# The norm ahead of the last feed-forward part: squares added on GpSimd, two sums on TensorE

## The chip, the cores and the metric

The kernel runs on one core of a Trainium2 chip. The time is the device time of one execution in microseconds. It runs as one program: TensorE (matrix products), VectorE, ScalarE, GpSimd (called POOL in the profile) and the DMA queues work side by side and wait for each other by semaphores that the code sets by hand.

## The reference, cut to what matters

Two transformer blocks on 512 tokens of 1024 features. The last part of the second block is what the change touches:

```
def rms_norm(x, g):
    y = x * rsqrt(mean(x * x, axis=-1) + 1e-6)
    return y * g

x = x + rms_norm(mem_attention(h, mem_n, ...), xa_post_g)     # "xapost"
h = rms_norm(x, ffn_pre_g)                                    # "ffnpre"
x = x + rms_norm(conv_ffn(h, w_up, conv_w, conv_b, w_down), ffn_post_g)

def conv_ffn(h, w_up, conv_w, conv_b, w_down):                # D_FF = 2816
    z = h @ w_up
    zc = conv_w[2] * z + conv_w[1] * shift_right(z, 1) + conv_w[0] * shift_right(z, 2) + conv_b
    g, u = zc[..., :D_FF], zc[..., D_FF:]
    return (gelu(g) * u) @ w_down
```

Everything is float32. The sum of squares over the 1024 features of each token, needed by "ffnpre", is what is computed in another way.

## The kernel before, in words

Activations lie with features on the partitions: eight tiles k = 0 to 7 of 128 features by 512 tokens (`xT[:, k, :]`). A float32 product is made of three products of rounded parts: weights and activations are each split into a high part (a rounded copy, made by ScalarE) and a low part (the value less the high part, made by VectorE), and TensorE multiplies high by high, high by low and low by high (lines 2422 to 2424, and 3288 to 3290). Weights come in units of 128x1024, loaded by the SP queue into four buffers `raw`, split by ScalarE (`hi`, line 587) and VectorE (`lo`, line 1382) into three buffers `whi` and `wlo`. A unit's buffer is free again when TensorE has used the unit three places before it.

The norm ahead of the feed-forward part is not applied before the product: TensorE multiplies `x * g`, and the factor rsqrt(mean) of each token is applied to the result in PSUM (`times_root`, on VectorE), when it is known. To have work early, the first four column blocks of `w_up` ("f2w", four PSUM banks) are done in 16 pieces, each one feature tile k of one half of the tokens (256 columns). `wide_order` is the order: tiles 0 to 5 of the first half, tiles 0 to 3 of the second, tiles 6 and 7 of the first, tiles 4 to 7 of the second. For piece n:

- VectorE: `half_norm(n)`, line 2126 (y1 times its gain times the factor of "xapost") and line 2128 (added to xT);
- ScalarE: `half_high(n)`, line 1278 (high part `h5h`) and line 1282 (square of xT into `tmp[k % 4]`). The square of a tile k >= 4 waits until the square four tiles before it in its half has been read (semaphore `p_sq`);
- VectorE: `half_low(n)`, line 2134 (low part `h5l`);
- TensorE: `half_wide(n)`, twelve products of 256 columns (3 for each of the four banks), and then line 3296, a product of a 128x128 matrix of ones with the square. It adds the squares over the 128 features of the tile, and over the eight tiles by accumulating in the bank "ffnpre". It raises `p_sq`, the last one `p_sum`.

The order in each engine's queue is written out by hand. On VectorE weight splits (`lo`) and the two steps of the second "xapost" factor (`newton`, lines 1394 and 1396) stand between the pieces; on ScalarE the weight copies (`hi`) and the roots. A matrix product with a float32 `ones` is issued as two instructions.

Before the pieces TensorE fills the four banks and the "ffnpre" bank with zeros by a product (line 3274), since every later product accumulates. Behind the pieces it goes on with the blocks ("f2g", jj) and ("f2u", jj), jj = 2 to 10, eight feature tiles of three products of 512 columns each. When `p_sum` is raised, ScalarE's `root("ffnpre")` (lines 601, 603, 609) and VectorE's `newton` make the factor, and then for each hidden block jj VectorE multiplies by it (line 2080), both engines compute the convolution (lines 1312, 2180, 2183), the gelu (1317), the product (2208) and the two parts of the result (1322, 2210), with weight splits in between.

`acc` is a 128x512 buffer in which VectorE has added squares for the two "xapost" sums; TensorE has read each half of it when `p_sum` stands at "xapost0" or "xapost1". GpSimd's last work is the scaling of the memory attention's probabilities (line 2396), before this stretch.

Of the kernel before, what the change touches and what calls it, by code (L numbers as in the profile page):

```python
# [12 lines left out]
ALU = mybir.AluOpType  # L13
# [181 lines left out]
def build(nc, ap, out):  # L195
# [4 lines left out]
    job = Order(JOBS)  # L200

    with ctx:
        def sem(name):
            return ctx.enter_context(nc.semaphore(name))
# [9 lines left out]
        def fix(name, shape, dt=F32):  # L214
            nonlocal o
            n = int(np.prod(shape)) * (1 if dt == U8 else 4)
            t = place(name, shape, dt, o)
            o += (n + 63) // 64 * 64
            return t
# [3 lines left out]
        ones = fix("ones", [128])  # L223
# [17 lines left out]
        tmp = [fix(f"tmp{i}", [512]) for i in range(4)]  # L241
# [9 lines left out]
        def work(name, shape, dt, kb):  # L251
            assert kb * KB + int(np.prod(shape)) * 4 <= WN, (name, kb, WN / KB)
            return place(name, shape, dt, W0 + int(kb * KB))
# [4 lines left out]
        def bank(b, n=512, c=0):  # L258
            return pall[:, 512 * b + c:512 * b + c + n]
# [71 lines left out]
        acc = work("acc", [512], F32, 124)  # L331
# [57 lines left out]
        s = Sems(*[sem("s_" + n) for n in Sems._fields])  # L389
# [54 lines left out]
        at = {n: i % 8 for i, n in enumerate(fills)}  # L444
# [71 lines left out]
        half_of = (slice(0, 256), slice(256, 512))  # L516
# [5 lines left out]
        wide_order = [(0, k) for k in range(6)] + [(1, k) for k in range(4)] + [(0, 6), (0, 7)] + [(1, k) for k in range(4, 8)]  # L522
# [1743 lines left out]
        def _(e):  # L2266
# [125 lines left out]
            for i in range(1, 16, 2):  # L2392
# [2 lines left out]
                w.wait_ge(s.drec, 64 + i + 1)  # L2395
                e.tensor_scalar(p, p, sd[:, c + 3:c + 4], None, ALU.mult).then_inc(s.pwg, 1)

        @block.tensor
        def _(e):
            w = Waits(e)  # L2400
            freed = {b: [] for b in range(8)}

            def fill(b):

                for sem_, value in freed[b]:
                    w.wait_ge(sem_, value)

            def unit(j):
                _, _, _, cn, _, nk, _ = plan[j]
                w.wait_ge(*lo_done(j))  # L2410
                return [t[j % 3][:, 0:cn * nk].rearrange("p (k c) -> p k c", c=cn) for t in (whi, wlo)]

            def gemm(keys, outs, ready, nk=8, between=None):

                k = 0
                for key in keys:
                    j = J[key]
                    a, b = unit(j)
                    for kk in range(plan[j][5]):
                        ready(k)  # L2420
                        for o_, xh, xl in outs:
                            e.matmul(o_, a[:, kk, :], xh(k), start=(k == 0), stop=False)  # L2422
                            e.matmul(o_, a[:, kk, :], xl(k), start=False, stop=False)  # L2423
                            mm = e.matmul(o_, b[:, kk, :], xh(k), start=False, stop=(k == nk - 1))  # L2424
                        k += 1
                        if kk == plan[j][5] - 1:
                            mm.then_inc(s.used, 1)
                        if between and k in between:
                            between[k]()
# [41 lines left out]
            for k in range(8):  # L2471
                mm = e.transpose(bank(3, 2, 2 * k), crow[0:2, 128 * k:128 * k + 128], ident[0:2, 0:2])
# [24 lines left out]
            for j in range(4):  # L2497
                w.wait_ge(s.sqs, j + 1)
                mm = e.matmul(bank(5), ones[:, :], xsq[2 * j][:, :], start=(j == 0), stop=(j == 3))
# [109 lines left out]
            def turn_keys(i):  # L2609
                z, hp = i // 2, i % 2  # L2610
                fill(6)
                fill(7)
                w.wait_ge(s.kdm, i + 1)
                for k, win_ in enumerate(windows[z][:5]):
                    to = bank(6, 128, 128 * k) if k < 4 else bank(7, 128)
                    t = e.transpose(to, ktd[:, hp, 128 * win_:128 * win_ + 128], ident[:, :])
                t.then_inc(s.kt, 1)
                freed[6] = [(s.ktk, 2 * i + 1)]
                freed[7] = [(s.ktk, 2 * i + 2)]
# [54 lines left out]
            def item_at(n):  # L2674
                if n in ITEM_AT:
                    item(ITEM_AT[n])

            for n in range(4):
                tokens("dv", 2 * n, range(6), rows(hxh, hch), rows(hxl, hcl), xc_ready,
                       between={4: lambda: item_at(n), 8: lambda: turn_keys(n)})  # L2680
# [16 lines left out]
            for i in range(4):  # L2697
                b = 2 * (i % 2)
# [3 lines left out]
                     between={2: lambda: key_sums(i - 1) if i else state(3), 5: lambda: item_at(4 + i)})  # L2702
# [42 lines left out]
            for i in range(4):  # L2745
                fill(i % 2)
                gemm([("gr", i, 0)], [(bank(i % 2),) + x_part], x_ready,
                     between={5 if i == 0 else 2: lambda: item_at(8 + i), 2 if i == 0 else 6: lambda: beside_r(i)})
# [6 lines left out]
            for i in range(3):  # L2755
                fill(DQ[i])
                between = {2: lambda: item_at(12 + i)}
# [149 lines left out]
            for m in range(3, 8):  # L2907
                b = wo_bank[m]
# [10 lines left out]
            for half in range(2):  # L2919
# [7 lines left out]
                for jj in range(2 if half == 0 else 11, 11 * half + 11):  # L2927
                    for i, g in enumerate(("f1g", "f1u")):
                        b = at[g, jj]
# [7 lines left out]
                for m in range(8):  # L2937
                    b = at["f1d", half, m]
# [15 lines left out]
            for k in range(0, 8, 2):  # L2954
# [3 lines left out]
                if k == 4:  # L2958

                    w.wait_ge(s.rstd, job["mixpre"])  # L2960
                    b = at["mixpre"]
# [7 lines left out]
            b = at["zf"]  # L2969
# [3 lines left out]
            for i in range(4):  # L2973
# [3 lines left out]
                if i == 0:  # L2977
                    b = at["ci"]
                    fill(b)
                    w.wait_ge(s.idb, 1 + 1)  # L2980
                    for qt in range(4):
                        mm = e.matmul(bank(b, 8, 8 * qt), cT[0:8, 128 * qt:128 * qt + 128], ident[0:8, 0:8], start=True, stop=True)
# [11 lines left out]
            for i in range(4):  # L2994
                b = at["pw", i]
# [4 lines left out]
                mm = e.matmul(bank(b), wl[:, i, :], plh[:, i, :], start=False, stop=True)  # L3000
# [108 lines left out]
            for m in range(8):  # L3109
                b = at["fb", m]  # L3110
# [9 lines left out]
            for m in range(8):  # L3120
                b = at["mo", m]
                fill(b)
                gemm([("mo", m, 0)], [(bank(b), lambda k: meh[:, k, :], lambda k: mel[:, k, :])], merged_ready,
                     between={4: lambda: mem_sums(6)} if m == 0 else None)
# [69 lines left out]
            for n in range(20):  # L3194
                if 0 <= n - 3 < 16:
                    i = n - 3
                    b = 2 + i % 2
# [6 lines left out]
                if n < 16:  # L3204
                    i, h, qt = mem_units[n]
                    b = i % 2
# [10 lines left out]
                if 0 <= n - 4 < 16:  # L3217
                    i, h, qt = mem_units[n - 4]
                    b = 4 + h % 2
# [5 lines left out]
                    for k in range(2):  # L3225
                        mm = e.matmul(bank(b)[:, qs], Vm[:, k, 128 * h:128 * h + 128], MT[i % 3][:, k, :],
                                      start=(k == 0), stop=(k == 1))
# [41 lines left out]
            post_sums(1)  # L3269

            zeros = identr[0:4, 4:5].to_broadcast([4, 128])
            for b in [at["f2w", i] for i in range(4)] + [at["ffnpre"]]:
                fill(b)
                e.matmul(bank(b), zeros, a[0:4, 0, :], start=True, stop=False)

# [4 lines left out]
            def half_wide(n):  # L3280
                sub, k = wide_order[n]
                a, b = unit(J["f2w", k - k % 2])
                h = half_of[sub]
                w.wait_ge(s.ul, 16 + n + 1)
                for i in range(4):
                    o_ = at["f2w", i]
                    c = slice(128 * i, 128 * i + 128)
                    e.matmul(bank(o_)[:, h], a[:, k % 2, c], h5h[:, k, h], start=False, stop=False)
                    e.matmul(bank(o_)[:, h], a[:, k % 2, c], h5l[:, k, h], start=False, stop=False)
                    mm = e.matmul(bank(o_)[:, h], b[:, k % 2, c], h5h[:, k, h], start=False, stop=(n == 15))  # L3290
                if sub and k % 2:
                    mm.then_inc(s.used, 1)

                o_ = at["ffnpre"]
                w.wait_ge(s.sq, 22 + 8 + n + 1)
                mm = e.matmul(bank(o_)[:, h], ones[:, :], tmp[k % 4][:, h], start=False, stop=(n == 15))
                mm.then_inc(s.p_sum if n == 15 else s.p_sq, 1)

            h5 = (lambda k: h5h[:, k, :], lambda k: h5l[:, k, :])
            for half in range(2):  # L3300
                if half == 0:
                    for n in range(16):
                        half_wide(n)
                    freed[at["ffnpre"]] = [(s.rsum, job["ffnpre"])]
                    for i in range(4):
                        freed[at["f2w", i]] = [(s.cv, 2 * (i % 2) + i // 2 + 1)]
                for jj in range(2 if half == 0 else 11, 11 * half + 11):
                    for i, g in enumerate(("f2g", "f2u")):
                        b = at[g, jj]
                        fill(b)  # L3310
                        gemm([(g, jj, 0)], [(bank(b),) + h5], fifth_ready)
                        freed[b] = [(s.cv, 2 * jj + i + 1)]

                def conv_ready(k):
                    w.wait_ge(s.flo, 22 + 11 * half + k + 1)

                for m in range(8 if half == 0 else 6):
                    b = at["f2d", half, m]
                    fill(b)
                    gemm([("f2d", half, m, 0), ("f2d", half, m, 8)],  # L3320
                         [(bank(b), lambda k: ch[:, k, :], lambda k: cl[:, k, :])], conv_ready, nk=11)
                    freed[b] = [(s.y, 16 + m + 1)] if half == 0 else [(s.yn, 24 + m + 1)]
# [150 lines left out]
```

## Time and profile before

| | us |
|---|---|
| median of 3 runs | 1578.89 (1578.67 to 1579.35) |
| the profiled execution | 1578.69, span 1576.9 |
| TensorE busy | 1539.9 (98%) |
| VectorE busy | 924.5 (59%) |
| ScalarE busy | 730.2 (46%) |
| GpSimd busy | 119.0 (8%) |

The span is the time from the first to the last instruction in the profile; the execution's own time is a little longer. Busy time counts when an engine has an instruction in work. TensorE's is modelled for pipelined products, so the distance from one start to the next is the better measure of what a product costs. "Idle before, releaser" in a row tells how long the engine stood still and what instruction's end let it go on.

### The profile page before, as it was taken

The page shows a single profiled execution, that of the slowest core. Times are in us where ns is not written, and L with a number is a line of the kernel's source. Part 1 is how long each engine was busy: PE and PEld are TensorE (multiplying, and loading weights), DVE is VectorE, ACT ScalarE, POOL GpSimd, SP SyncE. Part 2 cuts the span into 40 slices and gives each one's busy share as a digit, 9 for nine tenths or more (in the row PEclk, how much of TensorE's full clock was granted, in tenths as well). Part 3 has the DMA queues.
Part 4 walks back from the last instruction along what each step waited for, and adds up shares of the span by engine and source line. Part 5 has one row for each costly group of instructions (what it writes and reads, how often), then busy time and mean ns, then how long its engine had stood idle before and what let it go on. Part 6 is the DMA issues. An engine that isn't in the chain of part 4 may idle for free.

```text
span 1576.9 us, 19862 instructions
## 1 busy us (share of the span) xinstructions
PE 1539.9 (98%) x7947; PEld 1243.7 (79%) x7947; DVE 924.5 (59%) x1398; ACT 730.2 (46%) x1155; POOL 119.0 (8%) x105
## 2 busy tenths in 40 slices
PE   8999999999999999999999999999999999999998
PEld 5777876877888888888787677788679788888887
DVE  4866878977544333335646555366647785267745
ACT  5454456873422222333524667456465553244432
POOL 0000214630000000000100111120010000000000
PEclk9999999999999999999999999999999999999999
DMA  9731112025342332223222212233222232333231
GB/s 377 269 111 55 54 55 80 2 107 181 105 140 92 92 116 103 94 73 112 83 96 65 68 61 74 74 121 107 74 62 83 91 99 75 121 106 95 77 92 59
DMA packets 49841, 157.70 MB, mean 100 GB/s; under 512 B 5683, under 2 KB 12467, under 8 KB 49493
## 3 DMA queue, kind: packets, MB, share of 16 engines
q1 hardware_dynamic: 48352, 151.80, 29.7%
q10 hardware_dynamic: 1396, 4.63, 0.8%
q8 instruction: 63, 1.03, 0.3%
q14 instruction: 30, 0.24, 0.0%
HBM read 154.31 MB, written 2.10 MB: 99 GB/s over the span
## 4 chain that ended last, share of the span: by engine, by line
PE 83%; DVE 7%; ACT 7%; issue 2%; POOL 0%; DMA 0%; DVEq 0%; SPq 0%; ACTq 0%
PE pall L2422 18%; PE pall L2423 18%; PE pall L2424 18%; PE pall L3014 2%; PE pall L2456 2%; PE pall L2458 2%; PE pall L2457 2%; PE pall L3016 2%; PE pall L3015 2%; PE pall L2814 1%; DVE wlo L1382 1%; ACT whi L587 1%; PE pall L2855 1%; PE pall L2653 1%; PE pall L2842 1%
## 5 line engine op out<-in xcount | busy, mean ns | idle before, releaser
L1382 DVE TENSOR_TENSOR wlo<-raw,whi 128x1024 fp32r<-128x1024 f32 (+2 forms) x263 | 292.0, 1111 | 284.1 <-ACT whi L587 283.9
L587 ACT ACTIVATE whi<-raw 128x1024 fp32r<-128x1024 f32 (+2 forms) x263 | 247.0, 941 | 179.1 <-PE pall L2424 165.1
L2422 PE MATMUL pall<-h5h,whi 128*128 128x512 f32 x320 | 124.9, 390 | 1.0 <-DVE wlo L1382 1.0
L2424 PE MATMUL pall<-h5h,wlo 128*128 128x512 f32 x320 | 124.5, 389 | 0.0
L2423 PE MATMUL pall<-h5l,whi 128*128 128x512 f32 x320 | 124.5, 389 | 0.0
L2423 PE MATMUL pall<-h2l,whi 128*128 128x512 f32 x320 | 124.5, 389 | 0.0
L2424 PE MATMUL pall<-h2h,wlo 128*128 128x512 f32 x320 | 124.5, 389 | 0.0
L2422 PE MATMUL pall<-h2h,whi 128*128 128x512 f32 x320 | 124.5, 389 | 0.0
L2422 PEld LDWEIGHTS pall<-h5h,whi 128*128 128x128 f32 x320 | 60.1, 188 | 14.1 <-DVE wlo L1382 1.4
L2422 PEld LDWEIGHTS pall<-h2h,whi 128*128 128x128 f32 x320 | 60.1, 188 | 12.6
L2424 PEld LDWEIGHTS pall<-h5h,wlo 128*128 128x128 f32 x320 | 60.1, 188 | 12.6
L2423 PEld LDWEIGHTS pall<-h2l,whi 128*128 128x128 f32 x320 | 60.1, 188 | 12.5
L2424 PEld LDWEIGHTS pall<-h2h,wlo 128*128 128x128 f32 x320 | 60.1, 188 | 12.3
L2423 PEld LDWEIGHTS pall<-h5l,whi 128*128 128x128 f32 x320 | 60.1, 188 | 12.3
L2423 PE MATMUL pall<-fl,whi 128*128 128x512 f32 x176 | 68.5, 389 | 0.0
L2424 PE MATMUL pall<-fh,wlo 128*128 128x512 f32 x176 | 68.5, 389 | 0.0
L2422 PE MATMUL pall<-fh,whi 128*128 128x512 f32 x176 | 68.5, 389 | 0.0
L2424 PE MATMUL pall<-ch,wlo 128*128 128x512 f32 x154 | 59.9, 389 | 0.0
L2422 PE MATMUL pall<-ch,whi 128*128 128x512 f32 x154 | 59.9, 389 | 0.0
L2423 PE MATMUL pall<-cl,whi 128*128 128x512 f32 x154 | 59.9, 389 | 0.0
L1028 ACT ACTIVATE fh<-tmp 128x512 fp32r<-128x512 f32 x22 | 13.9, 632 | 95.1 <-DVE tmp L1870 95.1
L3014 PE MATMUL pall<-h3h,whi 128*128 128x512 f32 x120 | 50.2, 418 | 0.3 <-ACT tmp L1103 0.3
(531 smaller groups left out, 3650.9 us busy)
## 6 DMA issues: line engine op xcount, KB each, us to landing
raw<-in_weights SPq DMA_DIRECT2D x204, 512.0 KB, 3.5
mraw<-in_wmod SPq DMA_DIRECT2D x32, 512.0 KB, 5.1
mod<-in_weights SPq DMA_DIRECT2D x16, 512.0 KB, 14.6
raw<-in_weights SPq DMA_DIRECT2D x25, 256.0 KB, 2.6
raw<-in_weights SPq DMA_DIRECT2D x32, 192.0 KB, 2.4
xT<-in_x SPq DMA_DIRECT2D x4, 512.0 KB, 5.6
xT<-in_x ACTq DMA_DIRECT2D x1, 2048.0 KB, 7.7
out_y<-xT SPq DMA_DIRECT2D x5, 256.0 KB, 2.2
```

The lines of the kernel that those rows point to most:

```text
L587: e.activation(whi[j % 3][:, 0:cols(j)], raw[j % 4][:, 0:cols(j)], ACT.Copy).then_inc(s.hi, 1)
L1382: e.tensor_tensor(wlo[j % 3][:, 0:n], raw[j % 4][:, 0:n], f(whi[j % 3][:, 0:n]), ALU.subtract).then_inc(s.lo_v, 1)
L2422: e.matmul(o_, a[:, kk, :], xh(k), start=(k == 0), stop=False)
L2423: e.matmul(o_, a[:, kk, :], xl(k), start=False, stop=False)
L2424: mm = e.matmul(o_, b[:, kk, :], xh(k), start=False, stop=(k == nk - 1))
L2456: e.matmul(bank(o_), h_, a[:, kk, :], start=(k + kk == 0), stop=False)
L2457: e.matmul(bank(o_), h_, b[:, kk, :], start=False, stop=False)
L2458: mm = e.matmul(bank(o_), l_, a[:, kk, :], start=False, stop=(k + kk == 7))
L2653: mm = e.matmul(bank(6 + sub, 128, 128 * win_), lh[p, c], rh[p, c], start=True, stop=True)
L3014: e.matmul(bank(b), a[:, k, :], xh[:, k, :], start=(k == 0), stop=False)
L3015: e.matmul(bank(b), a[:, k, :], xl[:, k, :], start=False, stop=False)
L3016: mm = e.matmul(bank(b), c[:, k, :], xh[:, k, :], start=False, stop=(k == nk - 1))
```

## The change

GpSimd gets 16 instructions at the end of its queue. For piece n they wait for the square; the first of a half (tile 0) is a copy of the square into `acc`, after TensorE has read that half of `acc` for "xapost"; the other seven of a half add the square to `acc`. Each raises `p_sq`. TensorE's 16 products with `ones` (one a piece) become two, one for each half of the tokens: the first behind piece 13, the second inside the product ("f2g", 2), behind two of its eight feature tiles. The zero fill of the "ffnpre" bank goes, since each half is now written by a single product.

```
 @block.gpsimd, at its end
+            def square_sum(n):
+                sub, k = wide_order[n]
+                c = half_of[sub]
+                w.wait_ge(s.sq, 22 + 8 + n + 1)
+                if k == 0:
+                    w.wait_ge(s.p_sum, job[f"xapost{sub}"])
+                    e.tensor_copy(acc[:, c], tmp[0][:, c]).then_inc(s.p_sq, 1)
+                    return
+                w.wait_ge(s.p_sq, 14 + wide_order.index((sub, k - 1)) + 1)
+                e.tensor_tensor(acc[:, c], acc[:, c], tmp[k % 4][:, c], ALU.add).then_inc(s.p_sq, 1)
+
+            for n in range(16):
+                square_sum(n)

 @block.tensor
-            for b in [at["f2w", i] for i in range(4)] + [at["ffnpre"]]:
+            for b in [at["f2w", i] for i in range(4)]:
                 fill(b)
                 e.matmul(bank(b), zeros, a[0:4, 0, :], start=True, stop=False)
...
+            def before_sums(sub):
                 o_ = at["ffnpre"]
-                w.wait_ge(s.sq, 22 + 8 + n + 1)
-                mm = e.matmul(bank(o_)[:, h], ones[:, :], tmp[k % 4][:, h], start=False, stop=(n == 15))
-                mm.then_inc(s.p_sum if n == 15 else s.p_sq, 1)
+                h = half_of[sub]
+                if sub == 0:
+                    fill(o_)
+                w.wait_ge(s.p_sq, 14 + wide_order.index((sub, 7)) + 1)
+                mm = e.matmul(bank(o_)[:, h], ones[:, :], acc[:, h], start=True, stop=True)
+                if sub:
+                    mm.then_inc(s.p_sum, 1)
...
                     for n in range(16):
                         half_wide(n)
+                        if n == 13:
+                            before_sums(0)
...
-                        gemm([(g, jj, 0)], [(bank(b),) + h5], fifth_ready)
+                        gemm([(g, jj, 0)], [(bank(b),) + h5], fifth_ready,
+                             between={2: lambda: before_sums(1)} if (g, jj) == ("f2g", 2) else None)
```

## Rows read from the trace of the kernel before

**Rows 1.** The page, parts 1 and 4: busy time and chain by engine.

```profile
PE 1539.9 (98%) x7947; PEld 1243.7 (79%) x7947; DVE 924.5 (59%) x1398; ACT 730.2 (46%) x1155; POOL 119.0 (8%) x105
...
PE 83%; DVE 7%; ACT 7%; issue 2%; POOL 0%; DMA 0%; DVEq 0%; SPq 0%; ACTq 0%
```

**Rows 2.** Chain that ended last, in order of time: start us, us, what.

```profile
1221.73 0.45 PE pall L3296 x2
1222.20 0.70 ACT R L601
...
1254.74 1.13 DVE wlo L1382
1255.91 0.50 PE pall L2422
```

**Rows 3.** TensorE's waits, 1222 to 1577: who for whom, us in total, times, longest.

```profile
PE pall L2422 <- DVE wlo L1382: 1.0, 1, 1.0
PE pall L3375 <- DVE y L2235: 0.3, 1, 0.3
```

**Rows 4.** Timeline of TensorE: start us, us, engine, line, what, count, idle before.

```profile
1201.44 0.39 PE L3288 MATMUL pall<-h5h,whi 128*128 128x256 f32 x1 [0.15 <-DVE h5l L2134]
...
1202.97 0.59 PE L3296 MATMUL pall<-tmp,ones 128*128 128x256 f32 x2
...
1219.71 0.59 PE L3296 MATMUL pall<-tmp,ones 128*128 128x256 f32 x2
...
1221.57 0.59 PE L3296 MATMUL pall<-tmp,ones 128*128 128x256 f32 x2
...
1222.23 0.39 PE L2423 MATMUL pall<-h5l,whi 128*128 128x512 f32 x1
1222.46 0.40 PE L2424 MATMUL pall<-h5h,wlo 128*128 128x512 f32 x1
```

**Rows 5.** Busy by stretch: bounds, length, busy of five engines (count), clock, DMA.

```profile
1192.00:1197.00 5.00, 5.00 (x41) 4.83 (x41) 4.71 (x11) 3.83 (x10) 0.00 (x0) 1.00 0.31 105
1197.00:1209.00 12.00, 11.85 (x89) 11.12 (x88) 10.82 (x25) 7.30 (x17) 0.00 (x0) 1.00 0.14 45
1209.00:1217.20 8.20, 8.20 (x64) 7.98 (x63) 7.01 (x13) 3.83 (x9) 0.00 (x0) 1.00 0.34 94
```

**Rows 6.** Timeline of VectorE at the end of the pieces.

```profile
1209.08 1.22 DVE L1382 TENSOR_TENSOR wlo<-raw,whi 128x1024 fp32r<-128x1024 f32 x1 [0.77 <-ACT whi L587]
...
1213.85 1.23 DVE L1382 TENSOR_TENSOR wlo<-raw,whi 128x1024 fp32r<-128x1024 f32 x1 [0.77 <-ACT whi L587]
...
1216.70 0.48 DVE L2134 SCALAR_TENSOR_TENSOR h5l<-xT,vec,h5h 128x256 fp32r<-128x256 f32 x1
1217.36 0.48 DVE L2134 SCALAR_TENSOR_TENSOR h5l<-xT,vec,h5h 128x256 fp32r<-128x256 f32 x1 [0.18 <-ACT h5h L1278]
```

**Rows 7.** Timelines of VectorE and of GpSimd, 1018 to 1046.

```profile
1018.94 0.68 DVE L1382 TENSOR_TENSOR wlo<-raw,whi 128x512 fp32r<-128x512 f32 x1
...
1026.23 0.69 DVE L2016 TENSOR_TENSOR mel<-merged,meh 128x512 fp32r<-128x512 f32 x1
1026.84 1.78 DVE L1382 TENSOR_TENSOR wlo<-raw,whi 128x512 fp32r<-128x512 f32 x1
...
1023.69 1.29 POOL L2391 TENSOR_TENSOR merged<-merged,tmp 128x512 f32<-128x512 f32 x1 [1.03 <-DVE tmp L2023]
1026.40 1.68 POOL L2391 TENSOR_TENSOR merged<-merged,tmp 128x512 f32<-128x512 f32 x1 [1.42 <-DVE tmp L2023]
```

**Rows 8.** Timeline of GpSimd: two-input instructions of two sizes.

```profile
273.46 1.83 POOL L2318 TENSOR_TENSOR Kl<-Kd,Kh 128x768 fp32r<-128x768 f32 x1 [0.45 <-ACT Kh L879]
...
278.02 1.27 POOL L2344 TENSOR_TENSOR mixl<-rS,mixh 128x512 fp32r<-128x512 f32 x1 [1.79 <-ACT mixh L904]
```

**Rows 9.** Timelines around 895: a one-input instruction of GpSimd beside VectorE.

```profile
894.68 1.24 POOL L2388 TENSOR_SCALAR Pb<-Pb,statd 128x384 f32<-128x384 f32 x1 [6.53 <-DVE statd L1974]
...
895.11 1.23 DVE L1382 TENSOR_TENSOR wlo<-raw,whi 128x1024 fp32r<-128x1024 f32 x1 [0.32 <-ACT whi L587]
```

**Rows 10.** One line's instructions: ScalarE's squares of the pieces.

```profile
L1282 ACT ACTIVATE tmp<-xT x16: 400/402/403, 1190.9 to 1217.2; 128x256 f32<-128x256 f32 x16
```

## The prediction

> **What bounds the kernel now.** I read the page first: TensorE is busy 98% of the span and holds 83% of the chain that ended last, VectorE and ScalarE 7% each [rows 1]. That makes a removed product look like a gain, but it is an average, so I went on to the chain in the stretch of the change. There it leaves TensorE at the last of the sums (1221.73), goes to ScalarE's root at 1222.20, and from there runs for 33 us over VectorE and ScalarE (root, Newton step, the four convolutions of the first hidden blocks, the splitting of weights) until VectorE finishes the low half of a weight unit at 1255.87 and TensorE, which stood still, goes on at 1255.91 [rows 2]. The waits of TensorE behind the change say the same from its side: 1.0 us in one wait for exactly this, and in the whole rest of the span nothing else of size [rows 3]. So two things are to be seen. Whatever the change does to the time at which the sums are complete reaches the end of the kernel at full size, since behind 1255.91 TensorE is the bound and starts from there. And TensorE work saved before 1255.91 is worth nothing by itself: TensorE only comes earlier to the wait of [rows 3].
>
> **What sets the time of the sums.** They need the last of 16 token-half pieces. Each piece n is made by VectorE (norm: two instructions; low part: one) and ScalarE (high part, square), and TensorE then runs 12 products of 256 columns and now the sum. A unit with its sum is 1.86 us (1219.71 to 1221.57); a sum is 0.43 (the x2 of the chain, [rows 2]), so a unit without it is 1.43. A unit that had to wait takes 0.10 more: from 1201.44 to its sum at 1202.97 is 1.53 [rows 4]. VectorE is nearly full there: busy 4.71 of 5.00 us in 1192 to 1197 and 10.82 of 12.00 in 1197 to 1209, and 7.01 of 8.20 behind that [rows 5]; ScalarE has room.
>
> **TensorE's side of the change.** It removes 16 sums (16 x 0.43 = 6.9 us) and adds two (0.9), and removes one of five zero fills (at most a step of a 512-column product, 0.23 [rows 4], ahead of a wait for the first low part, so nothing). Take VectorE's times as they are for the moment. Low part 14 is ready at 1216.70 + 0.48 = 1217.18, low part 15 at 1217.84 [rows 6]. Without sums TensorE is early enough to wait for 14 (unit 13 with the first half's sum, which needs only the adds up to piece 11, is over by about 1216.5). Unit 14 starts at 1217.23 and takes 1.53, unit 15 takes 1.43, which gives 1220.19. The second half's sum now stands behind two steps of the next product, six matmuls at 0.23 [rows 4] = 1.38: 1221.57. That is to the hundredth where the last sum starts now [rows 4]. So the 6 us go three ways: TensorE waits longer for the low parts, gets 1.6 us ahead at 1220.19, and gives that back between there and 1255.91. Net on the time of the sums: 0.0.
>
> **POOL's side, which decides.** POOL gets two copies (pieces 0 and 6) and 14 adds of 128x256 with two inputs in SBUF. It stands still in this stretch now (0.00 busy, [rows 5]), so it has time enough; the question is what it does to VectorE. The trace has a pair that shows it. VectorE's weight split of 128x512, both inputs in SBUF, takes 0.68 us alone; begun at 1026.84 while POOL's two-input 128x512 add ran (1026.40 to 1028.08), it took 1.78 and ended 0.54 behind POOL's end [rows 7]. POOL's add in turn took 1.68 in place of the 1.29 of the one that met nobody: it began during a VectorE instruction that ended at 1026.91 and needed 1.17 from there [rows 7]. So these two shut each other out for the whole instruction, and an add of 512 columns costs a full VectorE 1.78 - 0.68 = 1.10 us.
> An add of 256 columns is not in the trace. From 128x768 (1.83) and 128x512 (1.27), 256 columns are 0.56 [rows 8]; the add is then 0.72 long, keeps VectorE out for 1.17 - 0.56 = 0.61 and costs it 1.10 - 0.56 = 0.54. Bounds: nothing, if all fell beside idle time of VectorE; 1.10, the price of the 512-column one, which no 256-column add should reach. A little is hidden where an add begins between two VectorE instructions that depend on each other; I take 0.50.
> All of VectorE's instructions of a piece have two inputs in SBUF (norm y and R, xT and y; low xT and h5h), as have the weight splits.
>
> How many adds count:
> - ScalarE runs 17 instructions in 1197 to 1209 [rows 5]: eight high parts, eight squares (pieces 4 to 11) and one weight part. Piece 6 is the copy, and the add of piece 11 falls in VectorE's wait of 0.77 for ScalarE at 1209.08 [rows 6]. Six adds, 6 x 0.50 = 3.0.
> - Adds 1 to 3 come in 1191 to 1197: 1.5, less VectorE's idle 0.29 there [rows 5] and about 0.2 in which piece 2 waits for ScalarE's root anyway: 1.0.
> - Adds 12 and 13 fall beside the waits for ScalarE of 0.77 at 1213.85 [rows 6] and a short one before it: 0. Adds 14 and 15 can delay only low part 15, which is needed 1.53 behind low part 14 and is ready 0.66 behind it: 0.
> Sum: low part 14, the one that TensorE waits for, comes 4.0 us later, and with it the sum (from 1221.57 to 1225.6), the root, and 1255.91 (to 1259.9). The bounds here are 0 and 12 x 0.55 = 6.6.
>
> The Trainium skill (SBUF — State Buffer, section on its two separate sides) calls this pair of ports an exclusive lock: a VectorE instruction with two SBUF inputs and a GpSimd one that reads SBUF block each other fully. The rows agree for two-input adds. It would hold for the two copies as well, which the rows speak against: VectorE's 128x1024 split of 1.23 us at 895.11, begun inside a one-input POOL instruction (894.68 to 895.92), took no longer than elsewhere [rows 9]. By the row the copies cost nothing, by the page they are a rival below.
>
> **Waits that are added.** ScalarE's square of a piece k >= 4 waits for POOL's add of piece k - 4 in its half, in place of TensorE's sum: four to six pieces back, done long before (0; queued behind it would be the high parts and the weight part). POOL waits for its own last add and for the first norm's sums, both early. TensorE's first sum waits for add 11, due some 5 us before; its second one for add 15: square 15 starts at 1217.2 now and takes 0.40 [rows 10], so it ends at 1217.6 + 4.0, the add by 1222.8, needed at 1225.6. The weight split due before the root moves along and is over before it. No DMA is moved; loads wait for VectorE's splits of four units before, with much time.
>
> **From the root on.** The chain of [rows 2] has no POOL work in it and moves as a block. TensorE has reached the unit of 1254.7 earlier than that and waits about 5 us in place of 1.0, some of it one unit before. Behind it nothing catches up, since TensorE is the bound to the end.
>
> Profiled execution: 1578.69 us (span 1576.9), and 1578.69 + 4.0 = 1582.7. The median 1578.89 of the three runs is 0.2 higher, inside their spread.
>
> **Rivals.**
> 1. The adds hardly hold VectorE up (its stride or size makes them fit between): then the sums come at 1222.2 as now, and the time is 1578.7. For it: POOL's one-input case [rows 9]. Against it: [rows 7]. It decides from the point where an add costs VectorE under 0.4 (8 x 0.4 = 3.2 is the limit of what can be told). This is the case on the other side, not slower. 17%.
> 2. The copies hold VectorE too: [rows 9] is a product with a column, and a copy may behave otherwise. Piece 6's copy falls in the full stretch, piece 0's before a weight split; each at most the price of an add: 4.0 + 2 x 0.5 = 5.0: 1583.7. 12%.
> 3. Every add counts in full, since POOL starts late behind its waits and misses the idle places: 12 x 0.55 = 6.6: 1585.3. 10%.
> 4. The saving on TensorE gets through: 14 x 0.43 + 0.2 = 6.2, 1572.5. Only if the chain of [rows 2] could start earlier by that, which low part 14 forbids; even its 1.6 us of lead are behind the wait of [rows 3]. 3%.
> The forecast has 58%, with its own range 1581.6 to 1583.8 (0.45 to 0.6 an add).
>
> **Numbers.** A change under 0.2% (3.2 us) can't be told from none. Slower by more: the forecast's share above 1582.1 (49 of its 58 points) and rivals 2 and 3: 0.71. Same: 9 points and rival 1: 0.26. Faster: 0.03. The range leaves out rivals 1 and 4 and reaches from a half-sized effect (about 1.3 us) to rival 3: 1580.0 to 1585.5.
>
> **What would show it.** VectorE's norm and low instructions (a low part is 0.48 now) longer by some 0.5 where a POOL add stands beside them, about nine or ten times; POOL's adds at 0.72 alone and up to 1.2 where they wait; the last low part at 1221.8 in place of 1217.84; the root at 1226.2; TensorE's wait for the weight split at 5 us. I am wrong if VectorE's durations stay at 0.48 (rival 1), if the root starts before 1224, or if TensorE's wait near 1255 is not the place where the lead ends.

## The result and the profile after

| | before | after |
|---|---|---|
| median of 9 runs, us | 1579.35 (1578.59 to 1580.74) | 1583.41 (1582.97 to 1583.67) |
| profiled execution, us | 1578.69, span 1576.9 | 1583.56, span 1581.8 |

The ratio is 1.0024 [1.0015, 1.0033]: the changed kernel is slower by 3.8 us, with an interval of 2.4 to 5.2. The ratio has its own estimate and is not quite the quotient of the two medians, here and below. The forecast was 1582.7.

The page of the changed kernel, span, busy time and chain, shows how little an average tells: TensorE has 4.4 us less to do than in [rows 1], the span is 4.9 us longer.

```profile
span 1581.8 us, 19834 instructions
PE 1535.5 (97%) x7918; PEld 1238.7 (78%) x7918; DVE 929.0 (59%) x1398; ACT 730.5 (46%) x1155; POOL 132.2 (8%) x121
PE 82%; DVE 9%; ACT 7%; issue 2%; POOL 0%; DMA 0%; DVEq 0%; SPq 0%; ACTq 0%
```

Next the stretch of the pieces: bounds, length, busy time of the five engines, clock, DMA. GpSimd now has work where it had 0.00 [rows 5], and VectorE is nearly full to the end of the pieces.

```profile
1192.00:1197.00 5.00, 3.49 (x25) 2.98 (x24) 4.92 (x9) 4.42 (x10) 2.33 (x3) 1.00 0.32 101
1197.00:1209.00 12.00, 9.03 (x69) 8.48 (x70) 11.56 (x21) 4.81 (x13) 5.04 (x7) 1.00 0.15 47
1209.00:1222.00 13.00, 10.37 (x79) 9.38 (x78) 11.49 (x21) 6.86 (x15) 5.02 (x7) 1.00 0.22 55
```

VectorE's three instructions of a piece, grouped by line over 1188 to 1224 (busy us, mean ns of one). The same 16 of each took 7.7, 6.8 and 7.7 us before. So 4.3 of VectorE's 4.5 us more on the page are in these 48 instructions.

```profile
L2134 DVE SCALAR_TENSOR_TENSOR h5l<-xT,vec,h5h 128x256 fp32r<-128x256 f32 x16 | 10.2, 645 | 0.5 <-ACT h5h L1278 0.5
L2128 DVE TENSOR_TENSOR xT<-xT,y 128x256 f32<-128x256 f32 x16 | 8.2, 511 | 0.6
L2126 DVE SCALAR_TENSOR_TENSOR y<-y,vec,R 128x256 f32<-128x256 f32 x16 | 8.1, 507 | 0.1
```

Which ones they are stands in the timelines (start us, us, engine, line, what, idle before). GpSimd first:

```profile
1192.33 0.59 POOL L2404 COPY acc<-tmp 128x256 f32<-128x256 f32 x1 [27.09 <-ACT tmp L1282]
1193.20 1.39 POOL L2407 TENSOR_TENSOR acc<-acc,tmp 128x256 f32<-128x256 f32 x1 [0.28 <-ACT tmp L1282]
...
1205.14 0.60 POOL L2404 COPY acc<-tmp 128x256 f32<-128x256 f32 x1 [1.19 <-ACT tmp L1282]
1206.41 0.74 POOL L2407 TENSOR_TENSOR acc<-acc,tmp 128x256 f32<-128x256 f32 x1 [0.67 <-ACT tmp L1282]
1208.36 0.92 POOL L2407 TENSOR_TENSOR acc<-acc,tmp 128x256 f32<-128x256 f32 x1 [1.21 <-ACT tmp L1282]
```

VectorE in the same time:

```profile
1192.58 1.42 DVE L1382 TENSOR_TENSOR wlo<-raw,whi 128x1024 fp32r<-128x1024 f32 x1
1193.92 0.95 DVE L2134 SCALAR_TENSOR_TENSOR h5l<-xT,vec,h5h 128x256 fp32r<-128x256 f32 x1
...
1205.39 0.62 DVE L2134 SCALAR_TENSOR_TENSOR h5l<-xT,vec,h5h 128x256 fp32r<-128x256 f32 x1
...
1206.44 0.98 DVE L2128 TENSOR_TENSOR xT<-xT,y 128x256 f32<-128x256 f32 x1
...
1208.60 0.96 DVE L2134 SCALAR_TENSOR_TENSOR h5l<-xT,vec,h5h 128x256 fp32r<-128x256 f32 x1
...
1213.92 1.22 DVE L1382 TENSOR_TENSOR wlo<-raw,whi 128x1024 fp32r<-128x1024 f32 x1 [0.56 <-ACT whi L587]
...
1221.54 0.48 DVE L2134 SCALAR_TENSOR_TENSOR h5l<-xT,vec,h5h 128x256 fp32r<-128x256 f32 x1
```

Read them in pairs. The add of 1193.20 waits for the weight split that ends at 1194.00 and is over itself at 1194.59; the low part queued behind the split ends at 1194.87 and takes 0.95 in place of 0.48. The add of 1206.41 meets no running instruction and is 0.74 long; the xT add of 1206.44 takes 0.98 in place of 0.42. The copies are shorter: the one of 1205.14 makes a low part 0.62, the one of 1192.33 makes the split 1.42 in place of 1.22. The last row is low part 14, for which TensorE waits; before, it began at 1216.70 [rows 6].

The chain of waits behind it (start us, us, what):

```profile
1221.62 0.41 DVE h5l L2134
1222.07 0.39 PE pall L3302
...
1226.58 0.45 PE pall L3314 x2
1227.05 0.70 ACT R L601
...
1259.60 1.14 DVE wlo L1382
1260.77 0.50 PE pall L2436
```

It is that of [rows 2]: the root at 1227.05 in place of 1222.20, TensorE let go at 1260.77 in place of 1255.91, 4.86 later. And TensorE's waits from 1188 to 1577 (us in total, times, longest):

```profile
PE pall L3302 <- DVE h5l L2134: 4.9, 6, 1.7
PE pall L3302 <- DVE wlo L1382: 2.2, 1, 2.2
PE pall L2436 <- DVE wlo L1382: 2.2, 2, 1.2
PE pall L3397 <- DVE y L2235: 0.3, 1, 0.3
```

The first two lines are 7.1 us of standing still within the pieces; the same view of before has 0.5 there. They hold the time that the missing sums free and, beside it, that VectorE comes later (without the adds they are 4.3, next section). The third line answers to the 1.0 us of [rows 3]; behind it nothing catches up.

**Where to measure from.** VectorE's first norm instruction of the pieces (line 2126) begins at 1189.47 before and at 1190.47 after: 1.00 us of the 4.86 is there before the change has done anything. The two kernels are the same up to there. The windows of 860 to 874 and 874 to 884 us show a short fall of TensorE's granted clock (sixth value behind the length, the last but two), in the first of them before and in the second after. Before:

```profile
860.00:874.00 14.00, 12.08 (x51) 7.93 (x51) 8.34 (x17) 10.78 (x20) 0.00 (x0) 0.88 0.30 92
874.00:884.00 10.00, 8.95 (x46) 6.55 (x45) 4.47 (x11) 7.22 (x14) 0.00 (x0) 1.00 0.10 30
```

After:

```profile
860.00:874.00 14.00, 11.85 (x56) 7.74 (x54) 8.84 (x19) 10.85 (x21) 0.00 (x0) 1.00 0.30 91
874.00:884.00 10.00, 7.98 (x33) 5.89 (x34) 3.59 (x9) 5.80 (x10) 0.00 (x0) 0.83 0.10 28
```

In the profiles of the experiments it is the same: the stretch starts at 1190.5 to 1190.7 where the fall is in the second window, and at 1189.4 to 1189.9 where it is in the first. So below times inside the stretch are given from its start, "rel.". Why the one shift goes with the other is not shown.

| rel. us | low part 14 begins | root begins |
|---|---|---|
| before | 27.23 | 32.73 |
| after | 31.07 (+3.84) | 36.58 (+3.85) |

With the 1.00 taken off, 3.86 are left of the 4.86 at TensorE's release, and from the start of the stretch to the end of the span it is 1391.3 us in place of 1387.4, 3.9 more. The two medians differ by 4.06.

### The profile page after: what moved, and what is told of

It is laid out like the page before. It is cut to its first block, busy times and chain, and to the rows that moved or that the text cites. A ratio compares the mean times of both kernels' runs of the same rounds, so it can differ in the third digit from the quotient of the medians.

```text
span 1581.8 us, 19834 instructions
## 1 busy us (share of the span) xinstructions
PE 1535.5 (97%) x7918; PEld 1238.7 (78%) x7918; DVE 929.0 (59%) x1398; ACT 730.5 (46%) x1155; POOL 132.2 (8%) x121
## 4 chain that ended last, share of the span: by engine, by line
PE 82%; DVE 9%; ACT 7%; issue 2%; POOL 0%; DMA 0%; DVEq 0%; SPq 0%; ACTq 0%
PE pall L2436 18%; PE pall L2438 18%; PE pall L2437 18%; PE pall L3028 2%; PE pall L2470 2%; PE pall L2472 2%; PE pall L2471 2%; PE pall L3030 2%; PE pall L3029 2%; DVE wlo L1382 1%; PE pall L2828 1%; ACT whi L587 1%; PE pall L2869 1%; PE pall L2667 1%; PE pall L2856 1%
```

## The experiments

Each ratio is to the kernel before, timed in the same rounds. Two theories were open: the adds hold VectorE up (mine), and, as rivals, that the waits or TensorE's new order do it, or that VectorE's longer durations are not what decides.

**One side at a time.** First, the change without the adds. What is left out is the adding, so TensorE's two sums are of a buffer that holds nothing of use:

```
-            for n in range(16):
-                square_sum(n)
 # ScalarE's square: the wait for p_sq of piece k-4 is gone
 # before_sums:
-                w.wait_ge(s.p_sq, 14 + wide_order.index((sub, 7)) + 1)
+                w.wait_ge(s.sq, 22 + 8 + wide_order.index((sub, 7)) + 1)
```

> TensorE's side of the change alone: GpSimd gets nothing, TensorE makes the two sums in their new places, from a buffer that holds no sum of these squares (the adding of the squares is left out), and the squares wait for nobody. Theory (GpSimd's adds shut VectorE out, TensorE's saving is lost): VectorE's low part 14 ready at 1217.2 as before, root 0.0 to 0.1 us from 1222.2, TensorE's wait for the weight split near 1255 grows from 1.0 to about 2.5, time within 0.5 us of before. Rival (TensorE's saving gets through, 14 x 0.43 + 0.2): 6.2 us faster. Second rival (the new place of the last sum, behind two feature tiles, costs by itself): root up to 1.4 us later, time 1.4 slower.

Measured: 1579.05 against 1579.62, 0.9996 [0.9987, 1.0005]. Low part 14 begins at rel. 27.23 and the root at 32.76, as before. The chain and TensorE's waits say where the saved 6.2 us went:

```profile
1222.22 0.45 PE pall L3312 x2
...
1222.69 0.70 ACT R L601
```

```profile
PE pall L3300 <- DVE h5l L2134: 2.8, 4, 1.3
PE pall L2434 <- DVE wlo L1382: 2.2, 2, 1.2
PE pall L3300 <- DVE wlo L1382: 1.5, 1, 1.5
PE pall L3395 <- DVE y L2235: 0.3, 1, 0.3
```

Most turned into waits: 4.3 us within the pieces, where it was 0.5 before, and 2.2 near 1255, where it was 1.0. TensorE's side of the change is worth nothing that these runs can tell.

Then the adds alone, in the kernel before, whose sums stay on TensorE:

```
+ # at GpSimd's end: square_sum(n) for 16 pieces as in the change,
+ # raising gadd in place of p_sq; nobody reads the result
+ # ScalarE's square of k >= 4: w.wait_ge(s.gadd, 8 + wide_order.index((sub, k - 4)) + 1)
+ # ScalarE's convolution (line 1312), which writes tmp again: w.wait_ge(s.gadd, 24)
```

> GpSimd's side alone: the kernel before, with its 16 sums on TensorE, and beside them the 16 GpSimd instructions of the change into a buffer that nobody reads. Theory: VectorE's part is delayed as in the changed kernel (norm and low instructions 0.35 to 0.5 longer some nine times, low part 14 about 3.9 later), the last sum 3.5 us later since TensorE has one sum more between unit 14 and 15 and no two feature tiles in front; time 3.5 slower than before (2.5 to 4.5). Rival (the loss comes from the sums' new places and waits on TensorE, not from the two engines' meeting in SBUF): no change, within 0.5 us.

Measured: 1582.47, 1.0016 [1.0007, 1.0025]; low part 14 at +3.82, root at +3.45. A GpSimd row and the VectorE row beside it:

```profile
1205.49 0.73 POOL L2409 TENSOR_TENSOR acc<-acc,tmp 128x256 f32<-128x256 f32 x1 [0.68 <-ACT tmp L1283]
```

```profile
1205.52 0.97 DVE L2130 TENSOR_TENSOR xT<-xT,y 128x256 f32<-128x256 f32 x1
```

These adds serve nobody, and they bring the whole delay of low part 14 and 3.45 of the root's 3.85. In time it is 2.6 us (1.1 to 4.0) of the 3.8, so the intervals leave room for a smaller part than the trace shows. The root comes 0.4 less late than in the changed kernel: here TensorE issues its sums as before.

**What kind of GpSimd instruction.** The add replaced by a copy of the square, and by a product with a column of `vec`; both have one wide input:

```
-                e.tensor_tensor(acc[:, c], acc[:, c], tmp[k % 4][:, c], ALU.add)
+                e.tensor_copy(acc[:, c], tmp[k % 4][:, c])                       # copies
+                e.tensor_scalar(acc[:, c], tmp[k % 4][:, c], v("ffn_pre_g_2", k), None, ALU.mult)   # column
```

> The changed kernel with every one of the 14 adds made a GpSimd copy of the square (one input in place of two; the adding is left out). In the changed kernel the two copies cost the VectorE instruction beside them 0.20 and 0.14 us. Theory (a copy holds VectorE too, but does not wait for it, and is 0.60 long): 8 or 9 that count at 0.15 to 0.2: 1.5 us slower than before (0.8 to 2.3). Rival a (only two-input instructions hold VectorE): no change from before. Rival b (a copy holds it as long as an add): 3.5 to 4 slower, as the changed kernel.

Measured: 1581.29, 1.0009 [1.0, 1.0017]. Low part 14 is at +1.36, as expected; the root's own +2.2 is not read here, since TensorE's clock fell in this stretch in the profiled execution (0.93 on average from 1198 to 1222).

> The changed kernel with every one of the 14 adds made a GpSimd product of the square with a column of gains (one tensor input and a column; the adding is left out). The trace of before has this kind beside VectorE's weight split at 894.68, and the split was not longer. Theory (this kind does not hold VectorE): GpSimd 0.92 each, VectorE's durations 0.48 and 0.42, time within 0.5 us of before. Rival (every GpSimd instruction that reads SBUF holds it for its length): 14 of 0.92 against 0.72 for an add, 5 us slower than before or more.

Measured: 1581.48, 1.001 [1.0001, 1.0019]; low part 14 at +1.55, root at +1.57. This expectation failed, and so did its rival of 5 us. The product is longer than the copy, but VectorE loses about the same. First the copies, then the column products:

```profile
1206.68 0.60 POOL L2407 COPY acc<-tmp 128x256 f32<-128x256 f32 x1 [1.19 <-ACT tmp L1282]
```

```profile
1206.93 0.62 DVE L2134 SCALAR_TENSOR_TENSOR h5l<-xT,vec,h5h 128x256 fp32r<-128x256 f32 x1
```

```profile
1204.49 1.16 POOL L2407 TENSOR_SCALAR acc<-tmp,vec 128x256 f32<-128x256 f32 x1 [0.69 <-ACT tmp L1282]
```

```profile
1204.86 0.62 DVE L2134 SCALAR_TENSOR_TENSOR h5l<-xT,vec,h5h 128x256 fp32r<-128x256 f32 x1
```

Both low parts take 0.62 in place of 0.48. The first pair (copies) is bounded by the copy's end at 1207.28; in the second (column products) the low part ends at 1205.48, before GpSimd's end at 1205.65. So the column product keeps VectorE out only in its first part. That may be why [rows 9] show no loss, where VectorE's instruction began 0.43 behind GpSimd's; no run tests that.

**Where the time can be had.** If the chain hangs on the sums, moving them earlier in the kernel before must help, and adding nothing on GpSimd. The sums of pieces 14 and 15 are issued behind unit 13's, ahead of units 14 and 15:

```
+                        for i in (13, 14, 15) if n == 13 else (n,) if n < 13 else ():
+                            half_sum(i)
```

> The kernel before with one thing moved: the sums of pieces 14 and 15 are made behind piece 13, ahead of the products of pieces 14 and 15. Nothing on GpSimd, the same 16 sums. It moves the root by a known amount the other way. Theory (the time of the root passes to the end until TensorE no longer waits for the weight split near 1255): root near 1219.2 in place of 1222.2, TensorE's wait of 1.0 (1.36 from last start to next less 0.23) gone, and no more than that: 1.1 us faster than before. Rival (the end does not hang on the root, since TensorE is 97% busy): no change. Second rival (all 3.0 us pass through): 3.0 faster.

Measured: 1577.6 against 1580.09, 0.9989 [0.998, 0.9997], which is 1.7 us (0.5 to 3.2). The time alone does not part 1.1 from 3.0. The trace does: the root begins 2.86 earlier, the wait near 1255 is gone from TensorE's list, and from the start of the stretch to the end of the span it is 1.4 us less (1386.0 against 1387.4):

```profile
1219.57 0.69 ACT L601 ACTIVATE R<-pall,small 128x512 f32<-128x512 f32 x1 [0.18 <-PE pall L3299]
```

```profile
PE pall L3288 <- DVE h5l L2134: 0.5, 2, 0.4
PE pall L3380 <- DVE y L2235: 0.3, 1, 0.3
```

Only the 1.0 us of that wait can be won by an earlier root; behind it TensorE is the bound. Now saved TensorE work should count, so next the squares and `ones` were rounded to the fast float32 form, which makes a sum one instruction instead of two, and sums 14 and 15 went behind piece 14 (ScalarE's square writes `sqr`, TensorE reads `sqr` and `onesr`; the last two lines are against the experiment above):

```
+        onesr = work("onesr", [128], F32R, 112)
+        sqr = [work(f"sqr{i}", [512], F32R, 104 + 2 * i) for i in range(4)]
-                        for i in (13, 14, 15) if n == 13 else (n,) if n < 13 else ():
+                        for i in (14, 15) if n == 14 else (n,) if n < 14 else ():
```

> The kernel before, with sums 14 and 15 behind piece 14, and all 16 sums as rounded float32 products (one matmul each, 0.12, in place of two, 0.43). GpSimd has nothing. TensorE loses 16 x 0.31 = 5.0 us of work and the root is 3.0 earlier. Theory: pieces stay bound by VectorE (low part 14 at 1217.2 after the stretch's start as before), TensorE reaches the next product 1.5 earlier and finds the weight split of 1255.9 ready: 1.1 + 1.5 = 2.6 us faster than before (2.0 to 3.2). Rival (TensorE's work counts in full): 5 us or more faster. Second rival (nothing before 1255.9 counts): within 0.5.

Measured: 1576.44, 0.9977 [0.9968, 0.9986], which is 3.6 us (2.2 to 5.1), more than the 2.0 to 3.2 expected, though the interval holds the 2.6; the root is at rel. 29.76, 2.97 earlier. A piece with its sum takes 1.56 in place of 1.86, so the sums free 16 x 0.30 = 4.8 us. TensorE waits 1.8 us within the pieces in place of 0.5, which takes 1.3 of them back, and in the profiled execution its clock fell there (0.68 over 1192 to 1197), which is another 1.6. The last step gives VectorE and ScalarE the two weight units of the stretch in another order, so that VectorE has work in the two waits of 0.77 of [rows 6]:

```
 ScalarE
-            for n in range(2, 12):
+            for n in range(2, 11):
...
+            half_high(11)
+            hi(J[("f2w", 6)] + 1)
 VectorE: lo(J[("f2w", 6)]) ahead of half_low(11), lo(J[("f2w", 6)] + 1) ahead of half_low(13)
```

> As e6, and in the queues of ScalarE and VectorE two weight splits (the last unit of the 16 pieces and the next one) are moved one to two instructions earlier, into places where VectorE waited 0.77 and 0.77 us for ScalarE. Theory (VectorE's row of instructions bounds the pieces, so that its idle time is what a change there can win): low part 14 about 1.9 earlier, TensorE at the next product 3.4 earlier than before, root 5 earlier, time 4.5 us faster than before (3.5 to 5). Rival (TensorE bounds the pieces once it waits less): as e6, 2.6 faster.

Measured: 1574.8 (five runs), 0.9968 [0.9956, 0.9981], which is 5.1 us faster than before (3.0 to 7.0; 3.5 to 5 was expected) and the best version found. Its slowest run, 1575.19, is below the fastest of the step before, 1576.02. Low part 14 begins 1.98 earlier, the root 4.75 earlier, and the two waits of 0.77 are down to one of 0.18:

```profile
1208.90 1.23 DVE L1386 TENSOR_TENSOR wlo<-raw,whi 128x1024 fp32r<-128x1024 f32 x1 [0.18 <-ACT whi L589]
...
1215.79 0.48 DVE L2138 SCALAR_TENSOR_TENSOR h5l<-xT,vec,h5h 128x256 fp32r<-128x256 f32 x1
```

```profile
1218.52 0.69 ACT L603 ACTIVATE R<-pall,small 128x512 f32<-128x512 f32 x1 [0.68 <-PE pall L3303]
```

**The order alone.** The same reorder was put into the changed kernel and into the kernel before.

> The changed kernel with the two weight splits moved to earlier places in the queues of ScalarE and VectorE, as in e7_reordered. Without GpSimd that move made low part 14 1.98 us earlier, since VectorE lost two waits of 0.77. In the changed kernel the adds of pieces 11, 12 and 13 lie beside those waits. Theory (an add costs nothing where VectorE is idle and 0.4 to 0.5 where it is not): the moved splits lay bare about three adds, so the move wins 1.98 - 3 x 0.4 = 0.8: low part 14 0.8 earlier than in the changed kernel, time 3.2 us slower than before (2.6 to 3.8). Rival (the adds cost the same wherever they fall): 1.98 earlier, 2.0 slower than before.

Measured: 1582.53 against 1579.55, 1.0021 [1.0012, 1.003]. The time is as expected, the step smaller: low part 14 is only 0.29 earlier than in the changed kernel, where 0.8 was expected. Three VectorE rows of it:

```profile
1211.24 0.97 DVE L2135 SCALAR_TENSOR_TENSOR h5l<-xT,vec,h5h 128x256 fp32r<-128x256 f32 x1
...
1216.24 1.76 DVE L1383 TENSOR_TENSOR wlo<-raw,whi 128x1024 fp32r<-128x1024 f32 x1
1217.92 0.94 DVE L2135 SCALAR_TENSOR_TENSOR h5l<-xT,vec,h5h 128x256 fp32r<-128x256 f32 x1
```

Once VectorE's idle places are filled, adds that fell into them cost about 0.5 each as well: what the order gives, the adds take.

> The kernel before with the two weight splits moved alone; TensorE keeps its 16 sums in their places. Theory (with a sum in each piece TensorE is the bound of pieces 6 to 15, at 1.86 us each, and VectorE has only to be early enough): low part 14 1.98 earlier, root and time as before within 0.3 us. Rival (VectorE bounds the pieces here as well): 1.9 faster.

Measured: 1579.79, 1.0001 [0.9992, 1.001]. The time came as expected, the step did not: low part 14 was 0.20 later. In this execution TensorE's clock fell to half inside the stretch,

```profile
1191.60:1195.00 3.40, 3.31 (x15) 3.22 (x15) 3.33 (x8) 3.34 (x9) 0.00 (x0) 0.51 0.37 92
```

and VectorE waited 1.50 for a weight copy at 1209.11 and 0.79 for a high part at 1213.23. On ScalarE's timeline both weight copies waited for TensorE, and that high part is queued behind the second one:

```profile
1208.02 1.06 ACT L587 ACTIVATE whi<-raw 128x1024 fp32r<-128x1024 f32 x1 [1.20 <-PE pall L3291]
...
1211.73 1.06 ACT L587 ACTIVATE whi<-raw 128x1024 fp32r<-128x1024 f32 x1 [1.95 <-PE pall L3291]
1212.70 0.49 ACT L1278 ACTIVATE h5h<-xT,vec 128x256 fp32r<-128x256 f32 x1
```

So in the kernel before, with 16 sums of two instructions on TensorE, the order may find nothing to win. The fall of the clock alone does not explain it: the profiled execution of the fastest version had it in the same place (0.66 over 1192 to 1197, here 0.69), and there low part 14 came 1.98 earlier. How much is the clock and how much TensorE's work, one profile can't tell; that stays open.

## Why the prediction was right

- *VectorE and GpSimd shut each other out, an add costs a full VectorE 0.5.* Right. Matched row by row up to low part 14, the adds lengthened eight VectorE instructions by 0.41 to 0.56 (four of them by 0.47) and two by 0.21 and 0.22, and part of that went into VectorE's waits for ScalarE, which shrank from 0.77 to 0.56. The add alone took 0.74 (forecast 0.72).
- *Low part 14 comes 4.0 later.* Measured 3.84, and 3.82 with the adds alone: the step holds, and the adds are the cause. That the sum came so near is in part luck. Read from start to start, adds 1 to 3 cost 1.18 (forecast 1.0); of the six adds in the middle five cost 2.34 and the sixth, beside the low parts ahead of VectorE's wait, went into that wait (forecast 3.0); the two copies cost 0.33 (forecast 0).
- *The forecast's own range, 1581.6 to 1583.8, for 0.45 to 0.6 an add.* Wrongly worked out: by the prediction's terms these prices give 3.55 to 4.9 us, 1582.2 to 1583.6. The lower end of the wide range is called a half-sized effect of 1.3 us; half of 4.0 is 2.0.
- *TensorE's side nets 0.0 on the time of the sums.* Right: root at +0.03 without adds, and 0.9996 in time. Rival 4 (6.2 faster) is out.
- *From the root on the chain moves as a block to the end.* Right: +3.85 at the root, +3.86 at TensorE's release. The profiled execution's other 1.00 us is upstream of the change.
- *The copies cost nothing.* Wrong. It rested on [rows 9], a pair that began too late to show it. The runs of copies and column products show 0.13 to 0.22 us for nearly each where VectorE is full; the two copies of the change cost 0.20 and 0.14, in place of the two times 0.5 of rival 2, which was right in kind. The rule of the Trainium skill (SBUF — State Buffer, section on its two separate sides), that a GpSimd instruction which reads SBUF and a VectorE one with two SBUF inputs block each other, is right in that one-input instructions block too; that they block for the whole instruction is not what the column product shows, where VectorE ended first.
- *TensorE waits about 5 us near 1255.* Wrong in size: 2.2, in two waits of 1.19 and 0.96. I let TensorE arrive early but forgot that it starts from low part 14, as late as everything else: 1.0 + 1.6 of lead - 0.43 for the second half's sum = 2.2. It did not enter the time. The 5 us and more that the change frees are where the first steps of the same part put them, in waits within the pieces (4.3 us without the adds, 7.1 with them and VectorE's delay).
- Rivals 1 and 3 are out with the first two points: an add costs more than 0.4, and not all twelve count in full.

## What to carry to other kernels

Before work is moved off the busiest engine, look at which engine the stretch itself waits for; here a 98% busy TensorE waited for VectorE, and 6 us less of its work were worth 0.9996 [0.9987, 1.0005]. Work put on an idle GpSimd is charged to a full VectorE, about 0.47 us for each add of 128x256 beside instructions with two inputs in SBUF. None of these experiments puts GpSimd beside VectorE instructions with one such input, so whether those are free is not shown. What paid was to issue the value on which the chain hangs earlier, then to cut TensorE's work, then to fill VectorE's idle places: 0.9989, 0.9977, 0.9968. The last step alone, in the kernel before, paid nothing (1.0001).

## What the runs showed of the hardware that was not expected

- A one-input GpSimd instruction of 128x256 delays VectorE as well, by 0.13 to 0.22 us (once 0.07), and about the same whether it lasts 0.60 (copy) or 1.16 (product with a column).
- A VectorE instruction that was kept out by an add or a copy ends at GpSimd's end plus its own length less 0.14 to 0.21: the low part beside the add of 1193.20 ends at 1194.87, 0.28 behind GpSimd's end at 1194.59, and is 0.48 long by itself (0.20 less); the split beside the copy of 1192.33 (ending at 1192.92) ends at 1194.00, 1.08 behind it, and is 1.22 long by itself (0.14 less).
- TensorE's granted clock falls to half for some 3.4 us at places that differ between executions, though the code up to there is the same: 0.51 in 1191.6 to 1195 in the profile of the kernel before with the new order, 1.00 in the same window of the kernel before. The profiles of three other experiments have it there too (0.66 to 0.68 over 1192 to 1197). Its place around 870 us goes with about 1 us in the start of the pieces.
